# Two silus and the token-major keys of an mLSTM tile, computed another way

## The reference

```python
cu = silu(causal_conv(u, conv_w, conv_b))        # 384 channels, 4 taps
q, k = cu per head @ wq * 96**-0.5, cu per head @ wk   # 4 heads of 96
# chunked mLSTM: decay weights from the i and f gates
s   = (q @ k.T) * exp(dmat - m)
num = w_inter * (C @ q) + s @ v
C_next = carry * C + sum_s ws * v_s k_s          # needs k by token
h   = num / max(|den|, exp(-m)), rms-normed
y_m = (h * g + skip * cu) * silu(mz)
y_a = sliding_window_attention(aq, ak, av, sinks) * silu(az)
y_s = stickbreaking(sq, sk, sv) * silu(sz)
x  += gate * rmsnorm(concat(y_m, y_a, y_s) @ w_out)
```

## Time and profile before

| | |
|---|---|
| median of 3 runs | 2435.57 us (2434.36 to 2437.19) |
| the profiled execution | 2434.36 us, span 2432.6 us |
| mean granted TensorE clock | 0.950 of full |
| busy over the span | PE 2169.0 us, DVE 1365.7, ACT 1102.9, POOL 541.1 |
| mix phase, first tile's first product to last tile's last transpose | about 1021 to 1865 us |
| from one tile to the next | 53.23 us (line 1424 at 1201.21 and 1254.44) |
| a DMA of one x tile (m_arena<-x, 512 KB) | 3.8 us from issue to landing |

### The profile page before, as it was taken

The page is one execution under the profiler, slowest core; times in us unless marked ns, Lnnn a source line. Parts: engine busy times, 40 slices in busy tenths (PEclk is TensorE's granted clock), DMA queues, the critical chain, the costliest instruction groups (busy, mean ns, idle before and its releaser), DMA issues. The chain is left out here.

```text
span 2432.6 us, 48778 instructions
## 1 busy us (share of the span) xinstructions
PE 2169.0 (89%) x20274; PEld 1545.0 (64%) x20274; DVE 1365.7 (56%) x2310; ACT 1102.9 (45%) x2358; POOL 541.1 (22%) x522
## 2 busy tenths in 40 slices
PE   1699999999999992399999999999995498998988
PEld 1466666666666661389999989999985143443433
DVE  6644443444444444644545544554542897988885
ACT  2343333343433331433334433344433497877784
POOL 0510000001000003023333333333332132322231
PEclk9799999999999996599999999999996699999999
DMA  9300000000000005500010000110002703021111
GB/s 399 124 21 21 18 19 27 19 19 27 19 18 27 18 10 190 207 22 29 28 41 26 25 29 29 28 41 25 26 20 74 248 1 111 11 75 48 61 53 53
DMA packets 82332, 139.02 MB, mean 57 GB/s; under 512 B 42432, under 2 KB 63040, under 8 KB 78016
## 3 DMA queue, kind: packets, MB, share of 16 engines
q1 hardware_dynamic: 82112, 135.79, 16.2%
HBM read 104.30 MB, written 31.46 MB: 56 GB/s over the span
## 5 line engine op out<-in xcount | busy, mean ns | idle before, releaser
L1310 PE MATMUL m_bank<-m_arena,m_w_hi 128*128 128x128 bf16 (+1 forms) x2560 | 444.5, 222 | 23.0 <-DVE m_w_lo L1282 22.3
L1311 PE MATMUL m_bank<-m_arena,m_w_hi 128*128 128x128 bf16 (+1 forms) x2560 | 444.0, 219 | 0.0
L1312 PE MATMUL m_bank<-m_arena,m_w_lo 128*128 128x128 bf16 (+1 forms) x2560 | 443.8, 219 | 0.0
L1310 PEld LDWEIGHTS m_bank<-m_arena,m_w_hi 128*128 128x128 bf16 (+1 forms) x2560 | 248.8, 97 | 29.0 <-DVE m_w_lo L1282 22.7
L1311 PEld LDWEIGHTS m_bank<-m_arena,m_w_hi 128*128 128x128 bf16 (+1 forms) x2560 | 254.1, 99 | 0.5
L1312 PEld LDWEIGHTS m_bank<-m_arena,m_w_lo 128*128 128x128 bf16 (+1 forms) x2560 | 248.1, 97 | 0.0
L1691 POOL TENSOR_TENSOR s_hi<-s_sp,s_cols 128x512 bf16<-128x512 f32 x144 | 152.3, 1057 | 366.2 <-DVE s_sp L1822 154.7
L218 POOL TENSOR_TENSOR g_stage<-g_stage,g_nh_row 128x1024 f32<-128x1024 f32 x16 | 52.3, 3268 | 735.4 <-DVE g_stage L487 735.4
L553 PE MATMUL g_bank<-g_wi_hi,g_h_hi 128*128 128x512 bf16 x512 | 194.2, 379 | 0.7 <-ACT g_stage L290 0.7
L554 PE MATMUL g_bank<-g_wi_lo,g_h_hi 128*128 128x512 bf16 x512 | 194.0, 379 | 0.0
L555 PE MATMUL g_bank<-g_wi_hi,g_h_lo 128*128 128x512 bf16 x512 | 194.0, 379 | 0.0
(11 more groups left out here) (361 smaller groups left out, 5451.4 us busy)
## 6 DMA issues: line engine op xcount, KB each, us to landing
m_arena<-in_w_in_dram SPq DMA_DIRECT2D x8, 1618.0 KB, 8.2
g_stage<-in_gla_w_in_dram SPq DMA_DIRECT2D x8, 1552.0 KB, 12.4
g_stage<-in_ada_w_dram SPq DMA_DIRECT2D x8, 1536.0 KB, 11.2
g_xs<-in_x_dram SPq DMA_DIRECT2D x16, 512.0 KB, 3.6
x<-g_stage SPq DMA_DIRECT2D x16, 512.0 KB, 2.7
m_arena<-in_w_mod_dram SPq DMA_DIRECT2D x8, 1024.0 KB, 7.0
m_arena<-x SPq DMA_DIRECT2D x16, 512.0 KB, 3.8
s_xr<-x SPq DMA_DIRECT2D x16, 512.0 KB, 4.1
```

The costliest lines, as they stand in the source:

```text
L1310: pe.matmul(out, l_hi, r_hi, start=(k == 0), stop=False)
L1311: pe.matmul(out, l_hi, r_lo, start=False, stop=False)
L1312: ins = pe.matmul(out, l_lo, r_hi, start=False, stop=(k == n - 1))
```

## The change

Five edits, all in `mix_phase`:

1. The conv's silu: ACT makes only Exp(-cv). DVE adds 1, takes the reciprocal and multiplies.
2. The outer gates: ACT's two passes over e_sb go. POOL adds 1 to e_sb; DVE takes the reciprocal, in its order after hh and ahead of the window sums; POOL multiplies as before.
3. k_tok, the keys in token order, comes from a product of cu and wk straight into B5, six pieces beside those of q and k, and no longer from transposes of kT. DVE's copy waits for qk_done.
4. `turn_x` of the next tile is issued in one piece behind the state product, and no longer in two halves around it.
5. `heads_out` no longer waits for skc_done.

```diff
# POOL
+                pool.wait_ge(s["sz_read"], i + 1)
+                pool.tensor_tensor(e_sb, e_sb, ones[:].broadcast_to([P, 1024]), ALU.add).then_inc(s["silu_one"], 1)
                 pool.wait_ge(s["silu_rec"], i + 1)
                 pool.tensor_tensor(z_sb[par], z_sb[par], e_sb, ALU.mult).then_inc(s["silu_done"], 1)
# ACT
-            ACT_LINKS = 9
+            ACT_LINKS = 6
...
-                link.done(act.activation(ec, cv, ACT.Exp, scale=-1.0))
-                link.done(act.activation(ec, ec, ACT.Ln, bias=one_col))
-                act.activation(ec, ec, ACT.Exp, scale=-1.0).then_inc(s["conv_exp"], 1)
+                act.activation(ec, cv, ACT.Exp, scale=-1.0).then_inc(s["conv_exp"], 1)
...
                 gate_out("sz", G0, P, (768, 1024), i, par)
-                act.wait_ge(s["sz_read"], i + 1)
-                link.done(act.activation(e_sb, e_sb, ACT.Ln, bias=one_col))
-                act.activation(e_sb, e_sb, ACT.Exp, scale=-1.0).then_inc(s["silu_rec"], 1)
# DVE
-            DVE_LINKS = 18
+            DVE_LINKS = 20
...
                 dve.wait_ge(s["hT_done"], i + 1)
-                dve.wait_ge(s["skc_done"], i + 1)
...
                 wait("qk_done", i)
+                link.done(dve.tensor_scalar(ec, ec, 1.0, None, ALU.add))
+                link.done(dve.reciprocal(ec, ec))
                 dve.tensor_tensor(cu, cv, ec, ALU.mult).then_inc(s["cu_done"], 1)
...
-                dve.wait_ge(s["ktok_turned"], i + 1)
+                dve.wait_ge(s["qk_done"], i + 1)
                 dve.tensor_copy(k_tok, ...)
...
                    .then_inc(s["hh_done"], 1)
+                dve.wait_ge(s["sz_read"], i + 1)
+                dve.wait_ge(s["silu_one"], i + 1)
+                dve.reciprocal(e_sb, e_sb).then_inc(s["silu_rec"], 1)
                 dve.wait_ge(s["p_done"], i + 1)
# TensorE
                     pe.matmul(B3[0:MD, hs], wq_sb[:, n, :], cu[:, b, :], start=first_b, stop=last_b)
-                    ins = pe.matmul(B4[0:MD, hs], wk_sb[:, n, :], cu[:, b, :], start=first_b, stop=last_b)
+                    pe.matmul(B4[0:MD, hs], wk_sb[:, n, :], cu[:, b, :], start=first_b, stop=last_b)
+                    ins = pe.matmul(B5[:, h * MD:(h + 1) * MD], cu[:, b, :], wk_sb[:, n, :],
+                                    start=first_b, stop=last_b)
                 ins.then_inc(s["qk_done"], 1)
...
-                wait("pT_copied", 3 * i)
-                for h in range(MH):
-                    ins = pe.transpose(B5[:, h * MD:(h + 1) * MD], kT[0:MD, h, :], ident[0:MD, 0:MD])
-                ins.then_inc(s["ktok_turned"], 1)
...
-                if not last:
-                    turn_x(i + 1, 0)
                 pe.wait_ge(s["ktok_copied"], i + 1)
...
                 if not last:
-                    turn_x(i + 1, 1)
+                    turn_x(i + 1)
```

More of the change, by code:

```diff
@@ L793, in mix_phase @@
                  "gates_done gates_read gate_abs u_done u_copied mz_done mz_read aqk_done aqk_copied tv_done tv_copied "
-                 "cols_done neg_max_done cols_exp az_done az_read qk_done qk_copied ktok_turned ktok_copied sqk_done sqk_copied "
+                 "cols_done neg_max_done cols_exp az_done az_read qk_done qk_copied ktok_copied sqk_done sqk_copied "
                  "qk_scores dx_arg dx_exp dx_done kv_done state_done sz_done sz_read inter_done intra_done "
@@ L797, in mix_phase @@
                  "scores_done hh_done max_done p_done pT_done pT_copied av_done oa_done oT_done ya_done ya_split "
-                 "rows_done silu_rec silu_done sqk_split ym_out ya_out sq_out sk_out sv_out sz_out dve_pre act_pre dve_link act_link "
+                 "rows_done silu_one silu_rec silu_done sqk_split ym_out ya_out sq_out sk_out sv_out sz_out dve_pre act_pre dve_link act_link "
                  "head_2_scored").split()
@@ L1335, in _, with turn_x @@
             pe.wait_ge(s["mod_out"], 1)
-            def turn_x(i, n):
+            def turn_x(i):
                 pe.wait_ge(s["xn_done"], i + 1)
[L1339 to L1347, removed]
+                for n, bank in enumerate((TR, B5)):
+                    if n == 0:
+                        wait("ya_done", i - 1)
+                        wait("cols_exp", i)
+                    else:
+                        wait("ktok_copied", i)
+                    for m in range(4):
+                        kb = 4 * n + m
+                        ins = pe.transpose(bank[:, m * T:(m + 1) * T], xn[:, kb * P:(kb + 1) * P], ident[:])
+                    ins.then_inc(s["xT_done"], 1)
             def turn_p(i, first):
@@ L1481, in tile @@
                 ins.then_inc(s["scores_done"], 1)
-            turn_x(0, 0)
-            turn_x(0, 1)
+            turn_x(0)
             pe.wait_ge(s["w_lo"], KB)
```

## The result

The changed kernel takes 2473.14 us (median of 4 runs, 2468.83 to 2474.91) against 2434.97 us before. The ratio is 1.0158 (95% interval 1.0142 to 1.0175): slower by 38 us, where 30 were forecast. Its profiled execution took 2479.82 us, span 2478.0. It is not among the four, and is 7 us above their median; three more executions on record took 2471.59, 2476.15 and 2479.27 us. The second profile (e10) shows what about half of such a difference is made of.

What follows compares the result with a forecast made beforehand. The prediction took TensorE to bound the middle phase. To the profiled 2434.36 us it added 15.2 for k_tok and 15 for the late gates, 2464.6, and named 2465 us for the median, range 2446 to 2485.

Steps and rivals of the forecast that it cites:

- What bounds the kernel: Middle phase: TensorE is the wall, busy 600.00 of 600 us; work taken from ACT is worth nothing by itself.
- k_tok: TensorE in each tile: 12 product instructions replace four transposes, net +0.95 us a tile, +15.2 us over 16 tiles.
- The conv's silu: DVE ahead of cu: reciprocal of 128x384 takes 2.46 us, with the +1 some 2.9, hidden under 10 us of cover.
- The wide reciprocal: DVE behind hh: the gates' 128x1024 reciprocal takes 6.3 us, by the slope of 6.0 ns a column in narrow rows.
- DVE 0.3 us earlier: DVE reaches hh 0.3 us earlier, since line 1152 runs without POOL's multiplication beside it: 1.22 us for 1.54.
- POOL's +1: POOL adds 1 to the gates in 2.35 us, done before anyone needs it.
- The wait: TensorE waits 1.0 us for ACT's copies of the probabilities at each tile handover but the first, 15 us in all.
- The clock: TensorE's granted clock inside the tiles: expected still at 0.99, no cost in the sum; a loss stood only in the second rival.
- the second rival: Reciprocal costs more than the slope, waits 2.0 us a tile, 2479.6 us; with clock falls 2505; longer reciprocal or clock 0.14.
- each of 15 waits: Clock part of the second rival: 1.7 us lost to the lower clock at every tile handover's wait, 25 us more.
- the sum as written: Whole kernel: 2434.36 us profiled, +15.2 for k_tok, +15 for the late gates, 2464.6; with 1.2 for the median, named 2465.

Runs made afterwards that it cites:

- e10: The changed kernel unaltered, run again for a second profile: 2470.28 us, ratio 1.0156 to the kernel before.
- e3: The kernel before with only the conv's +1 and reciprocal moved to DVE: 2433.06 us against 2432.68, ratio 1.0002.
- e1: The changed kernel with the gates' Ln and Exp back on ACT and the heads_out wait restored: 2446.69 us against 2433.72 for the kernel before.
- e2: The changed kernel with k_tok from transposes and turn_x in two halves again: 2455.22 us against 2433.72 for the kernel before.
- e4: The changed kernel with the gates' +1 and reciprocal in two pieces, columns 0 to 767 moved behind the k_tok copy: 2446.73 us, ratio 1.0053 to before.
- e5: The changed kernel with an extra, unused 128x128 reciprocal right ahead of the wide one: 2518.08 us, ratio 1.0346 to the kernel before.
- e9: The changed kernel with the gate columns moved inside the mv/av product, ahead of its last two blocks: 2474.95 us, ratio 1.0174 to the kernel before.
- e8: The kernel before with the gate columns moved inside the mv/av product, ahead of its last two blocks: 2428.92 us against 2432.68, ratio 0.9985.
- e6: The kernel before with p_times_v and the h transposes moved behind the mv/av product, right ahead of the gate columns: 2450.7 us against 2432.68.

## Why the prediction was right, and what it lacked

- **What bounds the kernel:** right. e3 took two activations off ACT and nothing moved.
- **k_tok:** right, a little high. Forecast 0.95 us a tile by the row with the same stationary block, 15.2 in all; e1 and before differ by 0.87 a tile and by 13.0 us in the medians. A piece of q, k and k_tok takes 0.635 us where q and k took 0.44, so 0.20 us for each product of two instructions, where the row gave 0.22.
- **The conv's silu:** right and hidden. The reciprocal took 2.56 us for 2.46; the +1 0.73 us, more than counted. cu was ready 1258.7.
- **The wide reciprocal:** 6.55 us for 6.3. The slope over all the narrow rows carried over to 1024 columns: (6546 - 178) / 1020 = 6.24 ns a column for 6.0. The Trainium skill (VectorE: DVE Perf Modes, Walkthrough: the 8-slice pipeline in each mode) gives Reciprocal a repeat count of 8; read as 8 cycles an element, it would have made 8.5 us, an estimate from that page. The trace does not agree.
- **DVE 0.3 us earlier:** right, 1.23 us for line 1149 with POOL silent.
- **POOL's +1:** 1.89 us for 2.35, of no effect.
- **The wait:** right in place and size, 14 of 1.06 us and one of 0.13 for 15 of 1.0; e2 shows it alone and e4 shows that only the place makes it. Left out: 0.2 us that TensorE loses around each, 3 us in all.
- **The clock:** this term was missing. The prediction gave "the clock still at 0.99" as a sign of being right, and held against the second rival that "a wait of 1 to 2 us is shorter than any that precedes a low clock in these rows". Both failed: the clock over that stretch is 0.98. 0.99 in the earlier trace rows was not full clock but three low stretches within 600 us, and they came with no wait at all. Even the 53.2 us that I called one tile held one: without one a tile takes 51.6 us. In the profiled execution 7 more stretches are 12 us. Falls right behind `p_times_v` came only in kernels with the wait (after, e5, e9, e10) and in none of the five that have the group in the same place without it (before, e1, e3, e4, e8). The falls behind the gate columns need no wait. Why some tiles have a fall and others with the same instructions have none is open.

The sum for the profiled execution over T: products 14.1, idle 14.7, around the waits 3.0, clock 11.9, together 43.7; T grew by 43.7. For the median, +38.2 less 13 + 15 + 3 leaves some 7 us for the clock; I estimate 4 more stretches, as many as the second profile has (7 for 3). So the forecast of 30 us lacked the last two terms. That it lies 8 us and not 10 from the measured 38 is a little luck: the products came out 2 us under their price. The clock's mechanism stood in part in the second rival, but at "each of 15 waits", 25 us; 4 to 7 stretches more is what came, and not all of them at waits. A slip of no effect: the sum as written, with the 1.2 us for the median, gives 2465.8 and not 2465.

## What to carry to other kernels

Where one engine is full, a slow operation on an idle engine is free only if nothing that the full engine will want is queued behind it in that engine's order: the same reciprocal cost 15 us and more behind hh, and nothing that the runs show when it was cut in two and three quarters of it moved ahead. For a matmul-bound kernel, look at the granted clock of stretches of a microsecond before calling a period steady, and price a wait of TensorE at its length, 0.2 us more, and a chance of the clock.

## What the runs showed of the hardware

- VectorE's reciprocal in f32 on 128 partitions took 948 ns for 128 columns, 1746 for 256, 2555 for 384, 4953 for 768 and 6546 for 1024: 6.2 to 6.3 ns a column between neighbouring sizes, and at 1024 columns five times the 1225 ns of the ordinary operation in the earlier trace rows.
- TensorE's granted clock fell to 1.2 GHz without any idle time. In the kernel before it did so about 1 us behind the thin group of lines 1406 to 1413, in 3 of 15 tiles, with TensorE busy on both sides:

```profile
1246.40:1248.60 2.20, 2.20 (x24) 2.07 (x24) 0.00 (x0) 2.02 (x6) 0.00 (x0) 1.00 0.03 7
1250.00:1252.50 2.50, 2.50 (x27) 2.50 (x25) 0.12 (x1) 0.63 (x1) 0.00 (x0) 0.50 0.00 0
1253.00:1254.00 1.00, 1.00 (x22) 1.00 (x19) 0.00 (x0) 0.00 (x0) 0.00 (x0) 1.00 0.00 0
```

  Putting thin groups side by side made 13 stretches of 3 (e6), breaking that group made 0 (e8). The order of the same instructions was worth 22 us (2450.7 against 2428.92).
- With a wait of 1.06 us ahead of the f32 group of `p_times_v`, the clock fell within 2.7 us of its end in 6, 2, 0 and 8 of 14 tiles (after, e10, e2, e9), and in 11 with a wait of 2.06 us (e5). Without the wait it did not fall there (before, e1, e3, e4, e8).
- An f32 product of 128x128 stationary and 96 moving columns ran in 0.20 us, two instructions.
